# Transformer layer on one core: rope tables ahead of the token tiles, first key norm behind the second tile's splitting

## The chip, the cores and the metric

The kernel runs on one core of a Trainium2 chip. The metric is the device time of one execution in microseconds (us). A core has TensorE (PE: matrix products, whose results go to PSUM banks; PEld are its weight loads), VectorE (DVE), ScalarE (ACT), GpSimd (POOL) and SyncE (SP), which issues nearly all the transfers here. The engines run their own instruction lists and wait for one another through semaphores.

## The reference, cut to what matters

One layer over 1024 latent tokens of width 1024 and 256 context tokens, all in float32:

```python
sh1, sc1, g1, sh2, sc2, g2 = modulation(c, w_mod, b_mod)          # silu(c) @ w_mod + b_mod, also for c_ctx
h_lat = rmsnorm(x, g_attn) * (1 + sc1) + sh1                      # context tokens: with their own shift and scale
z = h @ w_in                                                      # parts cq 256, ckv 128, kr 32, qs 512, ks 128, vs 128
q_m = rmsnorm(rmsnorm(cq, g_q_a) @ w_uq, g_mla_q)                 # 8 heads of 64 + 32
kv  = rmsnorm(ckv, g_kv_a) @ w_ukv                                # 8 heads: 64 for the key, 64 value
k_m = rmsnorm(concat(k_nope, broadcast(kr)), g_mla_k)
q_s, k_s = rmsnorm(qs, g_swa_q), rmsnorm(ks, g_swa_k)             # 8 heads and 2 heads of 64
# latent tokens: rotary embedding of the last 32 of q_m and k_m, and of q_s and k_s
mix = concat(mla_latent(...), swa_latent(...)); x = x + g1 * (mix @ w_out)
x = x + g2 * (relu(modulate(x) @ w_mlp1) ** 2 @ w_mlp2)
```

## The kernel before, in words

The kernel has four stages one after the other: tokens, attention, output projection, MLP. Only the token stage is touched. It ends near 240 us of 1422.

**Precision.** Products are made in three passes. Each float32 operand is split: a high part (ACT copies it into a type with fewer mantissa bits, F32R) and a low part (DVE subtracts: operand less high part), and TensorE sums high x high, high x low and low x high. So each weight has a job `high_weights(j)` on ACT and `low_weights(j)` on DVE; the jobs, in the order of `JOBS` (L264), are a0 and a1 (rows 0 to 3 and 4 to 7 of the 416 columns that keys and values come from), kv (w_ukv), r0 to r3 (a quarter each of the 768 other columns of w_in) and uq (w_uq). The low part of a0 is made by POOL (L455), counted on the semaphore `first_low`. The others are counted on `w_lo`. Each transposed tile is split in the same way by `hi_fill` (ACT) and `lo_fill` (DVE).

**Tiles.** The 1280 tokens are ten tiles of 128, tiles 0 and 1 context (`lat(t)` is false), 2 to 9 latent. What happens to a tile t:

- `square_x` (ACT) sums the squares, then root and inverse. For tiles 0 and 1 `root_x` and `inverse_x` do that for the tile alone, in `stx`. For a later tile its sum goes into column 26 of `stn` and takes part in the root and inverse of the norms of tile t - 2 (`variances`, `roots`, `inverses`).
- `scale_x` (DVE) multiplies with inverse and scale row; `add_shift` (POOL) adds the shift row. Tile 0 has `modulate_first` on DVE for both, straight from PSUM.
- TensorE transposes the tile in two halves (`fill` x0, x1), both are split, and `project(t, 0)` gives the 416 columns; latent tiles have `project(t, 1)` and `(t, 2)` for the other 768.
- `copy_z` takes the result to SBUF, `take_a` squares parts of it. The compressed part is transposed and split (`c`), and `up_kv` (latent: also `up_q`) multiplies with w_ukv (w_uq).
- Norm: `square_k`, `variances`, `roots`, `inverses`, then `scale_s`, `scale_q`, `scale_k`, `high_v` and `low_v`. POOL rotates (`rotate_keys`, `rotate_queries`) and spreads the rotated key over the heads (`widen_key`).
- The results are transposed again (`fill` s, sk, k0, k1, q0, q1), split, and stored to DRAM (`spill_...`).

**Order.** The order of each engine's work is written out by hand, as a loop over i from 0 to 10 in `gpsimd`, `scalar`, `vector` and `tensor`, with lap i making the projection of tile i and finishing tile i - 1. All transposes take turns in PSUM banks 0 and 1, in the order of `slot`: a transpose may start when the one two before it has been split (semaphore `emptied`). The tile 0 keys (sk, k0, k1 of 0) are transposed in lap 2, between the products of `project(2, 0)`. In lap 0, `spread_row(n)` makes TensorE copy scale and shift rows over all partitions; 0 to 3 are for context, 4 to 7 for latent tiles; `copy_spread(n)` brings them to SBUF, from the banks in `spread_bank` (L263). All four latent rows come ahead of tile 0's `fill("c", 0)`.

**Tables.** The cosines and sines come from DRAM (`rope`, 768 KB) and are multiplied on POOL with the norm gains, by `build_table`, three `tensor_tensor` each, for four tables in `tab`: one in lap 0 behind `rotate_keys(0)`, the other three in lap 1 behind `rotate_keys(1)`. The gains that contain the attention scale are made by DVE first (`gains_scaled`).

**Transfers.** `sync` issues, in this order: the column of c, six blocks of w_mod (1 MB each), tile 0, two blocks of w_mod, a0, tile 1, a1, norm columns and rows (`gains`), kv, r0, r1, rope, r2, r3, uq, then tiles as their buffer comes free and the results.

## Time and profile before

| | |
|---|---|
| median of 3 runs | 1425.94 us (1423.24 to 1425.99) |
| the profiled execution, time | 1423.98 us |
| its span, first to last instruction | 1422.2 us |
| PE busy | 1354.3 us (95%) |
| PEld | 1144.6 us (80%) |
| DVE | 959.3 us (67%) |
| ACT | 703.0 us (49%) |
| POOL | 479.5 us (34%) |
| mean granted TensorE clock | 0.989 |

Times in the rows below are microseconds from the start of the span. In a timeline each line is a run of like instructions of one engine: start, duration from the start of the first to the end of the last, line of the kernel, operation, output <- inputs with their sizes, count, and in square brackets the idle time of the engine just before with what ended it. An engine that sits inside an instruction longer than the operation needs has no idle time in this view. The granted clock is 1.00 for TensorE's 2.4 GHz and 0.50 for 1.2 GHz.

### The profile page before, as it was taken

What the parts mean: (1) busy time and instruction counts of PE and PEld (TensorE: products, weight loads), DVE (VectorE), ACT (ScalarE), POOL (GpSimd) and SP (SyncE); (2) the same over time, 40 slices, a digit from 0 to 9 for tenths busy, and PEclk for the clock granted to TensorE, in tenths of its full rate; (3) what the DMA queues carried; (4) which work ended last, traced back from release to release, by engine and by line L of the source; (5) the groups of instructions that cost most, each with busy time, mean ns of one, the idle gap of its engine ahead of it and who ended that gap; (6) DMA issues with size and microseconds to landing.
All of it is one profiled execution on the core that took longest, in us unless ns stands there. A gap on an engine that the chain in (4) does not pass through costs nothing.

```text
span 1422.2 us, 18829 instructions
## 1 busy us (share of the span) xinstructions
PE 1354.3 (95%) x7274; PEld 1144.6 (80%) x7274; DVE 959.3 (67%) x1327; ACT 703.0 (49%) x1339; POOL 479.5 (34%) x295
## 2 busy tenths in 40 slices
PE   5799997999999999999999999999999999999969
PEld 1588886888788998998888888888888888888857
DVE  1888776888877877785774646557465656637477
ACT  2656655777778776972223424333233324323321
POOL 2666563000099992501002304132140503223060
PEclk9899999999999999999999999999999999999989
DMA  9465657900146556201123112121210212121003
GB/s 376 153 176 167 163 170 253 279 1 1 51 169 204 182 145 188 69 1 45 45 65 128 30 30 89 30 74 30 89 30 15 89 30 76 29 89 30 30 29 119
DMA packets 116969, 141.33 MB, mean 99 GB/s; under 512 B 7672, under 2 KB 98680, under 8 KB 114064
## 3 DMA queue, kind: packets, MB, share of 16 engines
q1 hardware_dynamic: 116624, 140.08, 31.5%
q8 instruction: 58, 0.95, 0.3%
q14 instruction: 31, 0.25, 0.1%
q0 software_dynamic: 256, 0.05, 0.0%
HBM read 108.37 MB, written 31.74 MB: 99 GB/s over the span
## 4 chain that ended last, share of the span: by engine, by line
PE 75%; DVE 11%; ACT 9%; DMA 2%; issue 2%; SPq 0%; DVEq 0%; ACTq 0%
PE f_ps L2024 24%; PE f_ps L2259 21%; PE a_ps L1381 7%; PE o_ps L1736 6%; PE a_ps L1397 6%; PE a_ps L1425 5%; ACT s_pr L1476 3%; PE t_ps L943 2%; ACT s_pT L1486 2%; PE t_ps L932 2%; DMA t_wm<-in_w_mod 1%; DVE s_nmx L1559 1%; PE t_ps L958 1%; ACT l_pr L1493 1%; DVE l_nb L1564 1%
## 5 line engine op out<-in xcount | busy, mean ns | idle before, releaser
L2024 PE MATMUL f_ps<-h,f_w 128*128 128x512 f32 x1536 | 357.9, 389 | 0.4 <-DVE h L1802 0.3
L2024 PEld LDWEIGHTS f_ps<-h,f_w 128*128 128x128 f32 x1536 | 288.1, 188 | 60.7 <-DVE h L1802 0.7
L2186 DVE TENSOR_TENSOR mix<-mix,f_ps 128x512 f32<-128x512 f32 x208 | 136.3, 683 | 149.6 <-PE f_ps L2259 149.6
L2067 POOL TENSOR_TENSOR f_w<-f_w,f_g 128x1024 f32<-128x1024 f32 x32 | 81.8, 2577 | 393.2 <-DMA f_w<-in_w_mlp 345.8
L2259 PE MATMUL f_ps<-f_bh,f_ah 128*128 128x512 f32 x448 | 175.4, 391 | 13.2 <-DVE mix L2186 13.1
L2259 PE MATMUL f_ps<-f_bh,f_al 128*128 128x512 f32 x448 | 175.0, 391 | 0.0
L2259 PE MATMUL f_ps<-f_bl,f_ah 128*128 128x512 f32 x448 | 175.0, 391 | 0.0
L2104 ACT ACTIVATE f_a<-f_ps 128x512 f32<-128x512 f32 x64 | 38.2, 597 | 254.7 <-PE f_ps L2024 254.7
L1573 DVE TENSOR_TENSOR l_pT<-a_ps,l_pT 128x512 fp32r<-128x512 f32 (+1 forms) x192 | 109.0, 594 | 53.0 <-ACT l_pT L1486 52.9
L1381 PE MATMUL a_ps<-l_k,l_q 96*128 96x512 f32 (+1 forms) x576 | 136.4, 366 | 0.5 <-DVE l_mo L1594 0.5
L943 PE MATMUL t_ps<-w_in,t_h 128*128 128x416 f32 (+2 forms) x600 | 123.6, 351 | 0.0
L1486 ACT ACTIVATE l_pT<-a_ps 128x512 fp32r<-128x512 f32 (+1 forms) x192 | 95.0, 525 | 39.2 <-PE a_ps L1397 38.8
L2259 PEld LDWEIGHTS f_ps<-f_bh,f_ah 128*128 128x128 f32 x448 | 84.6, 189 | 31.6 <-issue 14.0
L1493 ACT ACTIVATE l_pr<-a_ps,l_nb 128x256 f32<-128x256 f32 (+1 forms) x128 | 100.4, 789 | 13.9 <-DVE l_nb L1564 11.4
L2158 DVE TENSOR_TENSOR f_al<-f_a,f_ah 128x1024 fp32r<-128x1024 f32 x40 | 61.5, 1538 | 66.5 <-ACT f_ah L2115 66.5
L1381 PEld LDWEIGHTS a_ps<-l_k,l_q 96*128 96x128 f32 x576 | 95.3, 189 | 12.4 <-DVE l_mo L1594 0.7
L943 PEld LDWEIGHTS t_ps<-w_in,t_h 128*128 128x128 f32 x600 | 97.5, 189 | 6.1 <-DVE t_h L717 0.5
L2259 PEld LDWEIGHTS f_ps<-f_bl,f_ah 128*128 128x128 f32 x448 | 84.7, 189 | 17.5
L2259 PEld LDWEIGHTS f_ps<-f_bh,f_al 128*128 128x128 f32 x448 | 84.5, 189 | 17.7
L1564 DVE TENSOR_REDUCE l_nb<-a_ps 128x1 f32<-128x1280 f32 x64 | 94.8, 1482 | 3.9 <-PE a_ps L1381 3.4
L1397 PE MATMUL a_ps<-ident,l_pr 128*128 128x128 f32 x640 | 94.3, 275 | 2.4 <-DVE l_pT L1573 1.4
L1425 PE MATMUL a_ps<-l_pT,l_v 128*128 128x256 f32 x640 | 91.4, 289 | 1.1 <-DVE mix L1587 0.6
(212 smaller groups left out, 2355.2 us busy)
## 6 DMA issues: line engine op xcount, KB each, us to landing
l_wg<-in_w_mod SPq DMA_DIRECT2D x8, 2048.0 KB, 8.5
f_w1r<-in_w_mlp SPq DMA_DIRECT2D x32, 512.0 KB, 4.1
f_w<-in_w_mlp SPq DMA_DIRECT2D x16, 1024.0 KB, 5.0
t_wm<-in_w_mod SPq DMA_DIRECT2D x8, 1024.0 KB, 12.7
scratch_k<-t_kT SPq DMA_DIRECT2D x20, 384.0 KB, 4.3
l_k<-scratch_k SPq DMA_DIRECT2D x8, 960.0 KB, 9.7
scratch_q<-t_qT SPq DMA_DIRECT2D x16, 384.0 KB, 5.0
l_q<-scratch_q SPq DMA_DIRECT2D x8, 768.0 KB, 6.6
```

Source lines behind the costliest of these rows:

```text
L943: ins = MM(ps[:, ZB + n % 2, 0:w], hT[a][:, k, :], w_in[x][:, k, ZC[c]], start=(k == 0 and i == 0), stop=(k == KC - 1 and i == 2))
L1381: last = MM(fps[:, a0:a0 + hi - lo], qT[b][:, a, qt * P:(qt + 1) * P], kT[b][:, w, lo:hi], start=(i == 0), stop=(i == 2))
L1397: last = nc.tensor.transpose(ps[:, TB + n % 2, c * P:(c + 1) * P], x, ident[:, :])
L1425: last = MM(ps[:, OB, 0:2 * P], vm[h % 2][:, t, :], flat(l_pT[half][:, u % 2, t, :, :]), start=(half == 0 and t == 0), stop=(half == 1 and ...
L1486: nc.scalar.activation(hi_lo(s, k)[0], turned(s, k), ACT.Copy).then_inc(hi_ready, 1)
L1493: nc.scalar.activation(l_pr[:, odd, lo:hi], fps[:, a0 + lo:a0 + hi], ACT.Exp, bias=nb[:, odd:odd + 1], accum_out=l_sums[:, i, m % NB, m // ...
L1564: V.tensor_reduce(nb[:, s % 2:s % 2 + 1], fps[:, (s % 2) * KALL:(s % 2 + 1) * KALL], AX.X, ALU.max, negate=True).then_inc(shift_ready, 1)
L1573: V.tensor_tensor(lo, turned(s, k), hi.bitcast(F32), ALU.subtract).then_inc(emptied, 1)
L1736: last = nc.tensor.matmul(ps[:, YB[t % 2] + half, :], mT[:, t % 2, a, k, :], w_out[w][:, k, half * BANK:(half + 1) * BANK], start=(k == 0 ...
L2024: last = nc.tensor.matmul(ps[:, b, :], w1[:, g % 2, w, k, :], h2[x][:, k, half * HB:(half + 1) * HB], start=(k == 0 and i == 0), stop=(k = ...
L2186: V.tensor_tensor(y, x, ps[:, bank_of(d, i, t), :].rearrange("p (k c) -> p k c", c=P), ALU.add).then_inc(added, 1)
L2259: last = nc.tensor.matmul(ps[:, b, :], op_a[s][x][:, f, t * P:(t + 1) * P], op_b[s][w][:, f, :], start=(i in (M1, M2, M5) and f == 0 and k ...
```

## The change

- SP: norm columns and rows ahead of the last two blocks of w_mod; rope ahead of kv, r0 and r1.
- POOL: all four tables before the loop, behind waits for `rope_loaded` and `gains_scaled`; the low part of a0 is no longer POOL's; in lap 1 `add_shift(2)` stands ahead of `widen_key(0)`.
- DVE: the gains are scaled ahead of the modulation row; the low part of a0 stands between the modulation row and `modulate_first`; in lap 0 the low part of r0, now behind the splitting of tile 1, an `inverse_x(2)` of its own and `scale_x(2)` stand ahead of the low part of r1; the norm of tile 0 (`finish(0)`) moves from the start of lap 1 to behind the splitting of tile 2, and the low part of r2 behind it.
- ACT: latent rows 6 and 7 are copied behind the splitting of tile 1; tile 2 gets `root_x(2)`; `square_k(0)`, `roots(0)`, `high_v(0)` and then the high part of r2 stand behind the splitting of tile 2.
- PE: rows 6 and 7 behind `up_kv(0)`, in banks 4 and 5; the keys of tile 0 behind k = 5, 6 and 7 of `project(2, 0)` (before: 1, 3 and 5).

```diff
-    stx = small("t_stx", [P, 2])
+    stx = small("t_stx", [P, 3])
-    spread_bank = (5, 6, 7, 3, 4, 5, 6, 7)
+    spread_bank = (5, 6, 7, 3, 4, 5, 4, 5)
@@ sync
         load_x(0)
+        sp.dma_start(cols[:, :], A["norm_cols"]).then_inc(gains, 16)
+        sp.dma_start(norms[:, :], A["norm_rows"]).then_inc(gains, 16)
         load_wm(KC - 2)
         load_wm(KC - 1)
         load_raw("a0")
         load_x(1)
         load_raw("a1")
-        sp.dma_start(cols[:, :], A["norm_cols"]).then_inc(gains, 16)
-        sp.dma_start(norms[:, :], A["norm_rows"]).then_inc(gains, 16)
+        sp.dma_start(rope[:, :, :], A["rope_rows"]).then_inc(rope_loaded, 16)
         load_raw("kv")
         load_raw("r0")
         load_raw("r1")
-        sp.dma_start(rope[:, :, :], A["rope_rows"]).then_inc(rope_loaded, 16)
@@ gpsimd
-        pool.wait_ge(w_hi, 1)
-        G.tensor_tensor(split_view("a0", 1), raw_view("a0"), split_view("a0", 0).bitcast(F32), ALU.subtract).then_inc(first_low, 1)
         pool.wait_ge(gains, 32)
...
+        pool.wait_ge(rope_loaded, 16)
+        pool.wait_ge(gains_scaled, 1)
+        build_table(0, 64, ROPE, b_mk[:, NOPE:QK])
+        build_table(2 * ROPE, 256, SD, b_sk)
+        build_table(2 * ROPE, 128, SD, b_sq)
+        build_table(0, 0, ROPE, b_mq[:, NOPE:QK])
         for i in range(NT + 1):
+            if i == 1:
+                add_shift(2)
             if i:
...
                 widen_key(i - 1)
-            if i + 1 < NT:
+            if i != 1 and i + 1 < NT:
                 add_shift(i + 1)
             if i < NT:
                 rotate_keys(i)
-            if i == 0:
-                pool.wait_ge(rope_loaded, 16)
-                build_table(0, 64, ROPE, b_mk[:, NOPE:QK])
-            if i == 1:
-                pool.wait_ge(gains_scaled, 1)
-                build_table(2 * ROPE, 256, SD, b_sk)
-                build_table(2 * ROPE, 128, SD, b_sq)
-                build_table(0, 0, ROPE, b_mq[:, NOPE:QK])
@@ scalar, the loop
-            if i:
+            if i > 1:
                 square_k(i - 1)
...
-            if i:
+            if i > 1:
                 roots(i - 1)
                 high_v(i - 1)
...
             if i == 0:
-                for n in range(4, 8):
-                    copy_spread(n)
-            if i == 1:
-                high_weights("r2")
+                copy_spread(4)
+                copy_spread(5)
...
             if i == 0:
-                square_x(2, stn[:, 0, 26:27])
+                copy_spread(6)
+                copy_spread(7)
+                square_x(2, stx[:, 2:3])
+                root_x(2)
                 high_weights("r1")
             if i == 1:
+                square_k(0)
+                roots(0)
+                high_v(0)
+                high_weights("r2")
                 high_weights("r3")
                 high_weights("uq")
@@ vector
+        def finish(t):
+            link.reach()
+            variances(t)
+            inverses(t)
+            scale_s(t)
+            if lat(t):
+                scale_q(t)
+            scale_k(t)
+            low_v(t)
         inverse_x(0)
+        (the three scalings of the gains, gains_scaled)
         dve.wait_ge(wm_used, KC)
...
         V.tensor_tensor(mo[:, :], mo[:, :], gm, ALU.mult).then_inc(mod_ready, 1)
+        dve.wait_ge(w_hi, 1)
+        V.tensor_tensor(split_view("a0", 1), raw_view("a0"), split_view("a0", 0).bitcast(F32), ALU.subtract).then_inc(first_low, 1)
         modulate_first()
...
         scale_x(1)
-        (the three scalings of the gains, gains_scaled)
         low_weights("kv")
         for i in range(NT + 1):
...
-            if i:
-                (the lines of finish(i - 1), with scale_x(2) behind inverses for i == 1)
+            if i > 1:
+                finish(i - 1)
             if 1 < i < NT - 1:
                 scale_x(i + 1)
-            if i < 2:
-                low_weights(("r0", "r2")[i])
...
             if i + 1 < NT:
                 lo_fill("x0", i + 1)
                 lo_fill("x1", i + 1)
-            if i < 2:
-                low_weights(("r1", "r3")[i])
+            if i == 0:
+                low_weights("r0")
+                inverse_x(2)
+                scale_x(2)
+                low_weights("r1")
             if i == 1:
+                finish(0)
+                low_weights("r2")
+                low_weights("r3")
                 low_weights("uq")
@@ tensor, the loop
-                project(i, 0, {1: ("sk", 0), 3: ("k0", 0), 5: ("k1", 0)} if i == NCT else {})
+                project(i, 0, {5: ("sk", 0), 6: ("k0", 0), 7: ("k1", 0)} if i == NCT else {})
             if i == 0:
-                for n in range(4, 8):
-                    spread_row(n)
+                spread_row(4)
+                spread_row(5)
...
-                    pe.wait_ge(spread_copied, 8)
+                pe.wait_ge(spread_copied, 8 if i else 4)
                 pe.wait_ge(emptied, slot["c", i] + 1)
                 up_kv(i)
+                if i == 0:
+                    spread_row(6)
+                    spread_row(7)
```

## Rows read from the trace of the kernel before

**Rows 1.** Chain of waits in order of time: start, duration, engine, tile, line.

```profile
66.14 3.39 DVE w_uq L705 x2
```

**Rows 2.** Timeline of TensorE: start, us, operation, count, idle time before it.

```profile
39.74 3.59 PE L990 MATMUL t_ps<-t_mo,ident 128*128 128x512 f32 x8
...
47.79 4.81 PE L943 MATMUL t_ps<-w_in,t_h 128*128 128x416 f32 x24
...
58.65 1.09 PE L932 MATMUL t_ps<-ident,t_x 128*128 128x128 f32 x4 [4.13 <-POOL t_x L404]
...
61.59 2.91 PE L971 MATMUL t_ps<-w_kv,t_c 128*128 128x512 f32 x6
64.30 1.61 PE L943 MATMUL t_ps<-w_in,t_h 128*128 128x416 f32 x6
...
69.92 0.64 PE L932 MATMUL t_ps<-ident,t_kn 128*96 128x128 f32 x4 [1.10 <-DVE t_sK L728]
...
74.58 0.41 PE L932 MATMUL t_ps<-ident,t_sn 128*128 128x128 f32 x2 [1.13 <-DVE t_sn L768]
...
87.05 5.78 PE L943 MATMUL t_ps<-w_in,t_h 128*128 128x416 f32 x33
```

**Rows 3.** Timeline of GpSimd (POOL), 30 to 73 us.

```profile
30.06 3.73 POOL L455 TENSOR_TENSOR w_in<-w_in_raw,w_in 128x1664 fp32r<-128x1664 f32 x1 [24.89 <-ACT w_in L494]
...
39.86 2.37 POOL L404 TENSOR_TENSOR t_x<-t_x,t_shift_c 128x1024 f32<-128x1024 f32 x1 [5.75 <-DVE t_x L685]
42.19 1.24 POOL L392 TENSOR_TENSOR t_krot<-t_z,t_tab 128x32 f32<-128x32 f32 x1
43.39 1.73 POOL L393 TENSOR_TENSOR t_krs<-t_z,t_tab 128x16 f32<-128x16 f32 x1
...
47.27 1.58 POOL L440 TENSOR_TENSOR t_tab<-t_rope,t_norms 128x256 f32<-128x256 f32 x3
...
62.55 9.91 POOL L440 TENSOR_TENSOR t_tab<-t_rope,t_norms 128x512 f32<-128x512 f32 x9
```

**Rows 4.** Timeline of VectorE (DVE), 35 to 70 us.

```profile
35.42 0.69 DVE L717 TENSOR_TENSOR t_h<-t_ps,t_h 128x512 fp32r<-128x512 f32 x1 [0.38 <-ACT t_h L511]
...
36.63 1.89 DVE L708 TENSOR_TENSOR w_in<-w_in_raw,w_in 128x1664 fp32r<-128x1664 f32 x1
...
39.93 3.38 DVE L701 SCALAR_TENSOR_TENSOR w_kv<-w_kv_raw,t_cols,w_kv 128x1024 fp32r<-128x1024 f32 x1
43.24 1.80 DVE L708 TENSOR_TENSOR w_in<-w_in_raw,w_in 128x1536 fp32r<-128x1536 f32 x1
...
49.45 1.76 DVE L708 TENSOR_TENSOR w_in<-w_in_raw,w_in 128x1536 fp32r<-128x1536 f32 x1 [1.72 <-ACT w_in L494]
51.13 0.68 DVE L742 TENSOR_REDUCE t_stn<-t_sqk 128x8 f32<-128x512 f32 x1
...
53.09 1.28 DVE L685 SCALAR_TENSOR_TENSOR t_x<-t_x,t_inv,t_scale_l 128x1024 f32<-128x1024 f32 x1
...
55.36 0.87 DVE L787 SCALAR_TENSOR_TENSOR t_vm<-t_ps,t_inv,t_vm 128x256 fp32r<-128x256 f32 x2
...
66.07 3.47 DVE L705 SCALAR_TENSOR_TENSOR w_uq<-w_uq_raw,t_cols,w_uq 128x768 fp32r<-128x768 f32 x2
```

**Rows 5.** Issue of the table's source (SP timeline), then its landing (DMA view).

```profile
26.96 1.01 SPq L355 DMA_DIRECT2D t_rope<-in_rope_rows  x1
...
t_rope<-in_rope_rows SPq DMA_DIRECT2D x1, 768.0 KB, 12.2
```

**Rows 6.** Stretches: busy per engine, TensorE clock, DMA share, GB/s.

```profile
35.00:40.00 5.00, 4.90 (x25) 4.79 (x26) 4.32 (x10) 4.18 (x8) 0.14 (x1) 1.00 1.02 411
...
60.00:65.00 5.00, 4.18 (x13) 3.58 (x14) 3.41 (x9) 3.39 (x5) 4.77 (x11) 0.50 0.08 28
65.00:70.00 5.00, 3.90 (x24) 3.43 (x23) 5.00 (x5) 3.13 (x7) 4.92 (x3) 1.00 0.00 0
```

**Rows 7.** Timeline of ScalarE (ACT): the square of tile 2.

```profile
46.90 1.05 ACT L480 ACTIVATE t_junk<-t_x 128x1024 bf16<-128x1024 f32 x1
```

More of the change, by code:

```diff
@@ L678, in scale_x @@
         def scale_x(t):
-            r = stx[:, t:t + 1] if t < 2 else inv[:, (t - 2) % 2, 26:27]
+            r = stx[:, t:t + 1] if t <= NCT else inv[:, (t - 2) % 2, 26:27]
             scale = scale_l if lat(t) else scale_c
@@ L828, in vector @@
         inverse_x(0)
+        dve.wait_ge(gains, 32)
+        dve.wait_ge(cleared, 7)
+        V.scalar_tensor_tensor(out=g_qk[0:NOPE, :], in0=cols[0:NOPE, 3:4], scalar=MLA_SCALE, in1=cols[0:NOPE, 4:5],
+                               op0=ALU.mult, op1=ALU.mult)
+        V.tensor_scalar(b_mq, b_mq, MLA_SCALE, None, ALU.mult)
+        V.tensor_scalar(b_sq, b_sq, SWA_SCALE, None, ALU.mult).then_inc(gains_scaled, 1)
         dve.wait_ge(wm_used, KC)
@@ L837, in vector @@
         scale_x(1)
-        dve.wait_ge(gains, 32)
-        dve.wait_ge(cleared, 7)
-        V.scalar_tensor_tensor(out=g_qk[0:NOPE, :], in0=cols[0:NOPE, 3:4], scalar=MLA_SCALE, in1=cols[0:NOPE, 4:5],
-                               op0=ALU.mult, op1=ALU.mult)
-        V.tensor_scalar(b_mq, b_mq, MLA_SCALE, None, ALU.mult)
-        V.tensor_scalar(b_sq, b_sq, SWA_SCALE, None, ALU.mult).then_inc(gains_scaled, 1)
         low_weights("kv")
@@ L849, in vector @@
                 lo_fill("k1", 0)
-            if i:
-                link.reach()
-                variances(i - 1)
-                inverses(i - 1)
-                if i == 1:
-                    scale_x(2)
-                scale_s(i - 1)
-                if lat(i - 1):
-                    scale_q(i - 1)
-                scale_k(i - 1)
-                low_v(i - 1)
+            if i > 1:
+                finish(i - 1)
             if 1 < i < NT - 1:
                 scale_x(i + 1)
-            if i < 2:
-                low_weights(("r0", "r2")[i])
             if i == 4:
```

## The prediction, made before the changed kernel ran

> **What bounds the kernel now.** I read first the table by engine and the 40 slices: TensorE (PE) is busy 95% of the span, and the only thin part besides the load of the modulation weights is the first tenth. Then the chain of waits, in order of time: from 87 us on it runs lap after lap over TensorE with small joints, while between 36 and 76 us it runs mostly over VectorE (DVE) splitting weights [rows 1]. Then TensorE's timeline of that stretch. The reader is to see its gaps: 4.13 us before the first transpose of tile 2, which waits for GpSimd's (POOL's) shift of that tile, 1.10 us at 69.92 before the transposes of tile 0's keys, second half, and 1.13 us at 74.58 before those of tile 1; from 87.05 the laps of latent tiles are full [rows 2]. The question for the whole change is therefore one number: by how much does the start of the fourth tile, 87.05, move? Behind it the same instructions follow in the same order, with no lap that could give time back.
>
> Last I read POOL and VectorE side by side. POOL's shift of tile 1 runs 39.86 to 42.23; VectorE's kv low part is entered at 39.93 and takes 3.38 us. POOL's next, an operation on 32 elements, takes 1.24 us and ends as that low part does; the one after it, on 16 elements, takes 1.73 us and ends with VectorE's r0 low part [rows 3, 4]. They take turns, one whole instruction each. The r1 low part at 49.45, with POOL idle, takes 1.76 us. And nine table products take 9.91 us at 62.55, where their own pace would give 6.9 (below), with 3.5 us of low parts of r3 and uq beside them: 6.9 + 3.5 = 10.4. Turns explain this; running beside each other doesn't.
>
> **The change part by part.**
>
> *DMA order.* The table's source landed at 26.96 + 12.2 = 39.2 us [rows 5]. It now has w_ukv and two quarters of w_in_r less ahead of it, 0.52 + 2 x 0.79 = 2.10 MB, at 411 GB/s [rows 6] 5.1 us: it lands at 34.1. Norm rows and columns (0.16 MB) go ahead of the last two modulation blocks: 0.4 us, I take 0.5 with the small packets, for everything on the modulation's path. SP issues all this some 10 us ahead of its landing, so its queue loses nothing.
>
> *Low part of a0 from POOL to VectorE.* It goes ahead of the first tile's modulation. Its high part is ready at about 30.4 (0.5 later); 1.9 us as for a1 [rows 4]; modulation can start at 32.35 instead of 30.7. The first tile is then transposed and split 1.4 us later, and the a1 low part starts at 38.1 instead of 36.63. POOL is rid of 3.73 us [rows 3], but it had nothing to do then. This 1.4 us is covered by what follows, which is later still; uncovered it would cost 1.4.
>
> *Tables ahead of the tiles: the main term.* All twelve products now stand on POOL before the shift of tile 1. Their pace, start to start: the first three (256, 128 and 128 elements) took 1.58 us; I take 0.70 for 256, 0.42 for 128 and 1.25 for 512. 2 x 1.25 + 6 x 0.70 + 4 x 0.42 = 8.4, with the joints 8.6. Alone that is 34.2 to 42.8. But VectorE enters four operations with both inputs in SBUF in that stretch: a1 low 1.75, kv low 1.1 (3.38 less the 2.3 that it stood), scaling of tile 1, as many elements, 1.1 once it has its turn, vs low 0.2: 4.15 us. By turns, the tables end at 46.9 and the shift of tile 1 (2.37) at 49.3. Before it ended at 42.23: 7.1 us later. Bounds: 45.2 with no turns at all; 50.3 if the rotation's small operations get between too.
>
> *What waits for it.* TensorE has the spread rows 4 and 5 (1.7) behind the first tile's projection, which ends at 41.1 with its 1.2 to 1.4 of delay, then tile 0's transpose, done at 43.3, then nothing for 6 us. In the idle time of the kernel before the clock fell to 0.50 (1.2 GHz), and it was back at 1.00 only after 65 us, when TensorE had worked almost without a gap since 60.82 [rows 2, 6]. So I take half clock from 49.3 to about 54: two transposes 1.1 us each (the row at 58.65), the kv product 2.7 (61.59 to 64.30) against the half of its 2.91 us row, some 1.5, at full clock, two spread rows 1.7 (four took 3.59 with the last one's tail). 49.3 + 2.2 + 2.6 + 1.7 = 55.8 for the start of tile 1's projection, which was 47.79. Here the two spread rows, moved behind kv, stand in front of the projection, and their copies on ScalarE (ACT) in front of the square of tile 2.
>
> *The second tile's chain and tile 2.* Spread row 7 is copied by 56.3; the square of tile 2 takes 1.2 [rows 7]; its root and inverse, now steps of their own, 0.6 (tile 1's stood between the split that ends at 36.11 and the a1 low part at 36.63); scaling 1.28 [rows 4]: 59.4, against 54.37 before. Then POOL's shift and the low part of r1 start together. POOL first: shift done at 61.8; VectorE first: 63.5. Before, the transposes behind it started at 58.65 [rows 2]. Tile 1's projection (4.8 us) ends at 60.6, so from there TensorE waits. Transposes, splitting and the kv product of tile 1 follow; tile 2's projection starts at 66.6 or 68.4, I take the middle, 67.5, against 64.30.
>
> *Norm of tile 0 behind the splitting.* VectorE is through with tile 2's splitting at about 66.8, a little ahead of the projection. The norm of tile 0 takes 3.8 us: from 51.13 to 56.23 less the 1.28 of scaling in between [rows 4]. Then r2 and r3, 1.76 each, and uq: 3.47 less the 1.75 in which two table products had the turn = 1.7. That is 9.0, with half a microsecond for turns with POOL's key rotation: 76.3; then the low part of the sK tile, 0.4: 76.7. TensorE needs that before it can transpose the second half of tile 0's keys, now after k = 7 of tile 2's projection, and everything behind it, the key norm of tile 1 as well, comes from here. Before it was 69.92. So 6.7 us later. From 69.92 to 87.05 the order of the work stays as it was, with the same waits (next late is tile 1's key norm for the transposes at 74.58, 4.66 us behind, as before).
>
> **Sum.** 87.05 becomes 93.8: +6.7 us. The profiled execution took 1423.98 (span 1422.2 and 1.8 around it); with 6.7 it is 1430.7. The median shown is 1425.94, 2.0 above that execution, so I state 1425.94 + 6.7 = **1432.6**.
>
> **The skill, weighed.** The VectorE rows above show turns with low parts that are plain tensor_tensor operations on fp32 [rows 3, 4]. The Trainium skill, "Advanced Engine Details and Errata", section VectorE Performance Modes, puts the interference on 2-port Vector instructions and lists tensor_tensor as having no such mode: by it the low parts and the tables would run side by side. "SBUF — State Buffer" of the Trainium skill, section on the two sides of SBUF, calls it an exclusive lock held for the whole instruction and counts in operations with two SBUF inputs. The traces bear out the second. What the first would make of the time is rival one.
>
> **Rivals.**
> 1. *No turns during the tables.* POOL's products or VectorE's operations slip past each other. Then tables to 42.8, shift to 45.2 (3.0 later than before), TensorE idle for 2 us only and at full clock, two transposes 1.3, kv 1.5, two rows 1.8: projection 1 at 49.8; copy 7 at 50.4, scaling of tile 2 done at 53.5, shift at 55.8 or 57.6; VectorE through with tile 2's splitting at 60.3 in either case (the low part of r1 stands there anyway). Plus 3.8 + 5.2 + 0.4 = 69.7, against 69.92. No change: 1425.7. For it: only that page. Against: three rows with durations of two to four times the operation's own and more. It is the bound on the good side of the main term.
> 2. *The splitting gains: faster.* One mechanism: before, VectorE's norm of tile 0 and the low parts of r2 stood between scaling and splitting, and TensorE sat 4.13 us waiting for tile 2. If the shift of tile 2 is done by 54 us, VectorE is through with its splitting by 57.5, and 57.5 + 3.8 + 5.2 + 0.4 = 66.9, 3.0 before 69.92: 1422.9. It decides at the end of the tables: each microsecond later than 40 us takes one of the three. For it: those waits are there. Against: the source doesn't land before 34 and the products alone need 8.6, so it needs products or a landing faster than any row shows.
> 3. *Worse.* VectorE first each time, half clock a second time in the wait for tile 2, POOL's rotations of tile 1 each behind a low part (as the 1.73 us row): 68.4 instead of 67.5, 1 us more of turns, 0.8 of clock: +9.5, 1435.4.
>
> **How the numbers follow.** Forecast (+5 to +8.5) 0.62, rival 1 0.13, rival 2 0.08, rival 3 0.09; 0.08 for something between rival 1 and the forecast (+3 to +5). 0.2% is 2.85 us, about what a measurement of this kernel can tell from no change. Slower takes the forecast, rival 3 and the part between: 0.79; same 0.13; faster 0.08. The forecast's own range is 1430.9 to 1434.5; the one given, 1425.2 to 1436, takes in rival 1.
>
> **What would show it.** Right: table products from about 34 us, some of 2 us and more, in turns with a1, the scaling and kv; shift of tile 1 ending near 49; a gap of some 6 us on TensorE before the first transpose of tile 1, clock 0.50 behind it; tile 1's projection at about 56; the low parts of r2, r3 and uq in a row up to 76; tile 3's projection at about 94. Wrong: tables done by 43, or a gap under 3 us there, or the keys of tile 0 transposed before 72; wrong as a whole if 87.05 hasn't moved by 3 us or if laps behind it have changed length.

## The result, and the profile after

The changed kernel is slower: 1430.69 us in the median of 7 runs (1427.81 to 1432.31), the kernel before 1425.99 (1423.24 to 1428.33, 7 runs beside it). The ratio is 1.0035 [1.0024, 1.0046], 5.0 us [3.4, 6.6]. Measured again with the last experiments it was 1.0036 [1.0023, 1.0050]. The prediction was 1432.6, +6.7: the direction is right, and the loss lies at the lower edge of the forecast's own +5 to +8.5 (1430.69 is just under its 1430.9).

The profiled execution of the changed kernel took 1432.31 us, span 1430.5, mean clock 0.978; that of the kernel before had span 1422.2 and clock 0.989. The 8.3 us between the spans are more than the kernels differ by: the changed kernel's profile is the slowest of its seven executions, the other's is faster than its median. I use the traces for places, the ratios for sizes.

TensorE's timeline of the changed kernel (start, duration, operation, count, idle time before it):

```profile
26.61 1.94 PE L989 MATMUL t_ps<-t_wm,silu 128*32 128x512 f32 x8 [0.58 <-DMA t_wm<-in_w_mod]
30.18 5.18 PE L1000 MATMUL t_ps<-t_mo,ident 128*128 128x512 f32 x8 [1.63 <-DVE t_mo L850]
...
37.21 3.29 PE L1014 MATMUL t_ps<-w_in,t_h 128*128 128x416 f32 x16 [0.34 <-DVE t_h L720]
...
48.83 1.94 PE L942 MATMUL t_ps<-ident,t_x 128*128 128x128 f32 x8 [4.47 <-POOL t_x L404]
50.42 2.91 PE L981 MATMUL t_ps<-w_kv,t_c 128*128 128x512 f32 x6
53.13 2.17 PE L1000 MATMUL t_ps<-t_mo,ident 128*128 128x512 f32 x4
54.73 5.09 PE L953 MATMUL t_ps<-w_in,t_h 128*128 128x416 f32 x24
...
62.92 1.11 PE L942 MATMUL t_ps<-ident,t_x 128*128 128x128 f32 x8 [2.01 <-POOL t_x L404]
63.79 2.77 PE L981 MATMUL t_ps<-w_kv,t_c 128*128 128x512 f32 x6
66.36 4.03 PE L953 MATMUL t_ps<-w_in,t_h 128*128 128x416 f32 x18
...
75.22 1.09 PE L942 MATMUL t_ps<-ident,t_kn 128*96 128x128 f32 x4 [3.06 <-DVE t_sK L731]
75.96 3.55 PE L953 MATMUL t_ps<-w_in,t_h 128*128 128x256 f32 x15
80.32 0.66 PE L942 MATMUL t_ps<-ident,t_sn 128*128 128x128 f32 x2 [0.81 <-DVE t_sn L771]
80.63 4.42 PE L953 MATMUL t_ps<-w_in,t_h 128*128 128x256 f32 x15
...
94.65 5.54 PE L953 MATMUL t_ps<-w_in,t_h 128*128 128x416 f32 x31
```

Read it against [rows 2]. Two waits have changed for the worse: there is now one of 4.47 us for the shift of tile 1, and the one for the sK low part, 1.10 us before, is 3.06 at 75.22. The wait for tile 2 has gone from 4.13 to 2.01. The fourth tile starts at 94.65, before at 87.05. GpSimd shows why tile 1 is late, VectorE what took turns with it, and what stands ahead of the sK tile:

```profile
34.05 12.21 POOL L440 TENSOR_TENSOR t_tab<-t_rope,t_norms 128x256 f32<-128x256 f32 x12 [11.97 <-DMA t_rope<-in_rope_rows]
46.33 2.35 POOL L404 TENSOR_TENSOR t_x<-t_x,t_shift_c 128x1024 f32<-128x1024 f32 x1
...
58.99 3.79 POOL L404 TENSOR_TENSOR t_x<-t_x,t_shift_l 128x1024 f32<-128x1024 f32 x1 [7.77 <-DVE t_x L688]
```

```profile
38.75 2.72 DVE L711 TENSOR_TENSOR w_in<-w_in_raw,w_in 128x1664 fp32r<-128x1664 f32 x1
41.39 1.75 DVE L688 SCALAR_TENSOR_TENSOR t_x<-t_x,t_stx,t_scale_c 128x1024 f32<-128x1024 f32 x1
43.06 1.74 DVE L704 SCALAR_TENSOR_TENSOR w_kv<-w_kv_raw,t_cols,w_kv 128x1024 fp32r<-128x1024 f32 x1
...
58.82 1.75 DVE L711 TENSOR_TENSOR w_in<-w_in_raw,w_in 128x1536 fp32r<-128x1536 f32 x1
...
69.50 3.47 DVE L711 TENSOR_TENSOR w_in<-w_in_raw,w_in 128x1536 fp32r<-128x1536 f32 x2
72.90 1.94 DVE L708 SCALAR_TENSOR_TENSOR w_uq<-w_uq_raw,t_cols,w_uq 128x768 fp32r<-128x768 f32 x2
74.76 0.41 DVE L731 TENSOR_TENSOR t_sK<-t_ps,t_sK 128x256 fp32r<-128x256 f32 x1
```

The chain of waits of the changed kernel (start, duration, what) goes through just these:

```profile
18.22 15.70 DMA t_rope<-in_rope_rows
...
46.33 2.36 POOL t_x L404
...
58.99 3.80 POOL t_x L404
...
69.59 3.39 DVE w_in L711 x2
72.98 1.86 DVE w_uq L708 x2
```

Stretches of the changed kernel (busy us per engine with counts, then the granted clock, DMA share, GB/s):

```profile
20.00:25.00 5.00, 2.63 (x16) 0.20 (x8) 0.69 (x5) 2.63 (x4) 0.38 (x2) 0.50 1.03 422
...
70.00:75.00 5.00, 2.17 (x15) 1.71 (x13) 5.00 (x5) 4.82 (x9) 4.87 (x4) 0.92 0.44 131
75.00:80.00 5.00, 4.29 (x19) 3.97 (x19) 3.36 (x10) 1.49 (x4) 1.47 (x4) 0.50 0.41 106
80.00:85.00 5.00, 4.68 (x18) 4.18 (x19) 4.89 (x8) 2.64 (x11) 2.52 (x2) 0.56 1.01 281
```

and the kernel before, in the same columns:

```profile
20.00:25.00 5.00, 3.17 (x16) 0.38 (x16) 0.32 (x2) 2.63 (x4) 0.00 (x0) 1.00 1.00 414
...
80.00:85.00 5.00, 5.00 (x32) 4.44 (x31) 3.17 (x7) 3.14 (x7) 3.53 (x10) 1.00 0.37 95
```

The changed kernel has half clock (0.50, 1.2 GHz) in two stretches where the kernel before had full clock: during the modulation products, and behind the keys of tile 0. Neither was in the prediction.

### The profile page after: what moved, and what is told of

Same layout as the page of the kernel before. It is cut to its first block, busy times and chain, and to the rows that moved or that the text cites. A ratio compares the mean times of both kernels' runs of the same rounds, so it can differ in the third digit from the quotient of the medians.

```text
span 1430.5 us, 18832 instructions
## 1 busy us (share of the span) xinstructions
PE 1362.8 (95%) x7274; PEld 1152.7 (81%) x7274; DVE 955.7 (67%) x1330; ACT 704.0 (49%) x1340; POOL 478.9 (33%) x294
## 4 chain that ended last, share of the span: by engine, by line
PE 75%; DVE 10%; ACT 8%; DMA 2%; issue 2%; SPq 1%; POOL 1%; DVEq 0%; ACTq 0%; POOLq 0%
PE f_ps L2037 24%; PE f_ps L2272 21%; PE a_ps L1394 7%; PE o_ps L1749 6%; PE a_ps L1410 6%; PE a_ps L1438 5%; ACT s_pr L1489 3%; PE t_ps L953 2%; ACT s_pT L1499 2%; PE t_ps L942 2%; DVE s_nmx L1572 1%; DMA t_rope<-in_rope_rows 1%; PE t_ps L968 1%; ACT l_pr L1506 1%; POOL t_tab L440 1%
## 5 line engine op out<-in xcount | busy, mean ns | idle before, releaser
L953 PE MATMUL t_ps<-w_in,t_h 128*128 128x416 f32 (+2 forms) x600 | 127.3, 359 | 0.0
L953 PEld LDWEIGHTS t_ps<-w_in,t_h 128*128 128x128 f32 x600 | 100.7, 196 | 6.3 <-issue 0.5
```

The source lines that it names most:

```text
L953: ins = MM(ps[:, ZB + n % 2, 0:w], hT[a][:, k, :], w_in[x][:, k, ZC[c]], start=(k == 0 and i == 0), stop=(k == KC - 1 and i == 2))
```

## The experiments

Two theories stood at the outset. By the prediction's, all of the loss comes from the tables ahead of the tiles, and the norm of tile 0 behind the splitting only passes it on. By its rival, the norm's new place costs something of its own. A third came up with the traces: that the norm rows ahead of the last modulation blocks bring on the half clock at the start. Twelve kernels ran, four on the same chip each time, most of them 12 times. Ratios are against the kernel before on that chip (medians 1425.63, 1425.72 and 1424.56 us). One microsecond is 0.0007.

### Tables back in the laps

```diff
@@ gpsimd
-        pool.wait_ge(rope_loaded, 16)
-        pool.wait_ge(gains_scaled, 1)
-        build_table(0, 64, ROPE, b_mk[:, NOPE:QK])
...
         for i in range(NT + 1):
...
                 rotate_keys(i)
+            if i == 0:
+                pool.wait_ge(rope_loaded, 16)
+                build_table(0, 64, ROPE, b_mk[:, NOPE:QK])
+            if i == 1:
+                pool.wait_ge(gains_scaled, 1)
+                build_table(2 * ROPE, 256, SD, b_sk)
+                build_table(2 * ROPE, 128, SD, b_sq)
+                build_table(0, 0, ROPE, b_mq[:, NOPE:QK])
```

> The changed kernel with the four tables built where they were before (one behind the first tile's key rotation, three behind the second's), all else changed. Theory (the tables ahead of tile 1's shift are the cost, by taking turns with VectorE's low parts and by standing in front): the shift of tile 1 ends at about 44 us instead of 48.7, tile 1's projection starts near 49 instead of 54.7, the second half of tile 0's keys is transposed near 71 instead of 75.2 (the three tables now take turns with the low parts of r2, r3 and uq): about 1427, 3 to 5 us under the changed kernel. Rival (the moved norm of tile 0 and the low part of a0 on VectorE are the cost, and the tables are hidden): within 1 us of the changed kernel, 1430.7.

Measured: 1428.40 us (1425.31 to 1432.16, 12 runs), 1.0022 [1.0010, 1.0035]. By the ratios only 1.9 us of the 5.0 come back, and the two intervals overlap; 3.1 us of loss stay, clear of zero. Tile 1's projection starts at 49.07 (changed: 54.73), so the tables' chain is gone, but the loss isn't. TensorE waits behind it:

```profile
70.04 0.64 PE L944 MATMUL t_ps<-ident,t_kn 128*96 128x128 f32 x4 [3.55 <-DVE t_sK L733]
...
77.04 0.66 PE L944 MATMUL t_ps<-ident,t_sn 128*128 128x128 f32 x2 [3.61 <-DVE t_sn L773]
```

Three tables now run on GpSimd from 71.35 to 78.39, beside tile 1's key norm on VectorE, and delay that in turn.

### Tables ahead, and nothing else

```diff
@@ the kernel before; sync and the scaling of the gains as in the changed kernel; gpsimd
+        pool.wait_ge(rope_loaded, 16)
+        pool.wait_ge(gains_scaled, 1)
+        build_table(0, 64, ROPE, b_mk[:, NOPE:QK])
...
         for i in range(NT + 1):
...
                 rotate_keys(i)
-            if i == 0:
-                pool.wait_ge(rope_loaded, 16)
-                build_table(0, 64, ROPE, b_mk[:, NOPE:QK])
...
```

> The kernel before with only the tables ahead of the tile loop, and what they need for it: norm rows and table source earlier in SP's order, and the gains scaled ahead of the modulation row. Norm of tile 0, spread rows and low part of a0 as before. Theory: the tables delay the shift of tile 1 by 6 us, tile 1's projection starts near 54, three tables less stand beside the low parts of r3 and uq (2 us back): 1430 to 1431, the loss of the whole change. Rival (the moved norm is what costs): within 1 us of before, 1426.

Measured: 1428.08 us (1426.80 to 1429.64, 11 runs), 1.0023 [1.0014, 1.0032]: 3.3 us. Tables from 34.47 to 48.18, shift of tile 1 done at 50.60, tile 1's projection at 54.31. It is slower on its own, but by less than the loss of the whole change, 1430 to 1431, that I expected here.

### Tables early, made from the norm rows

This kernel leaves out the cosines and sines, and with them the wait for their transfer:

```diff
-        pool.wait_ge(rope_loaded, 16)
-            G.tensor_tensor(..., rope[:, :, src + o:src + o + w], mid(g, NB), ALU.mult)
+            G.tensor_tensor(..., mid(norms[:, o:o + w], NB), mid(g, NB), ALU.mult)
```

> The changed kernel with the table products made from the norm rows, which land at 21.6 us, in place of the cosines and sines: same number, size and place of products, but they start at about 24 us, when VectorE is nearly idle (so the output isn't the reference's). Theory of turns: the twelve take about 8.6 us plus at most one low part (a0, 1.9) and the modulation row's product (0.7), against 12.2; POOL is free by 35, tile 1's shift ends near 43.5, and the whole is 6 to 8 us under the changed kernel, about 1423.5. Rival (no turns, a table product is slow for its broadcast operand or its strided output): 12.2 us again at 24, still done by 36.5, same gain of time but the group's length tells. Rival (tables are not the cost): 1430.7.

Measured: 1428.07 us (1423.48 to 1430.06, 12 runs), 1.0015 [1.0003, 1.0027]. The tables are out of the way before tile 1, and 2.1 us of loss stay, where I had expected none. This execution also gives the tables' own pace. GpSimd, then VectorE beside it:

```profile
24.33 10.68 POOL L440 TENSOR_TENSOR t_tab<-t_norms 128x256 f32<-128x256 f32 x12 [2.47 <-DVE t_norms L846]
```

```profile
29.11 1.37 DVE L849 TENSOR_TENSOR t_mo<-t_mo,t_bg 128x512 f32<-128x512 f32 x1
30.41 2.41 DVE L851 TENSOR_TENSOR w_in<-w_in_raw,w_in 128x1664 fp32r<-128x1664 f32 x1
```

Taken one by one, the products that meet no such VectorE operation last about 0.72, 0.45 and 1.27 us (256, 128 and 512 elements) in this kernel and in the changed one; from start to start that makes 8.6 us for the twelve, the prediction's figure. So the turns cost GpSimd 2.1 us here and 3.6 in the changed kernel. VectorE's operations beside them last, alone, 2.6 (0.69 and 1.89) and 4.75 (1.89, 1.28, 1.28 and 0.30). They do take turns, and each turn costs GpSimd 0.2 to 0.4 us less than VectorE's operation lasts alone: the product entered at 31.03, beside the low part of a0 (1.89), stood 2.37 us for its 0.72. The other theory, a product slow for its operands, is out.

### Low part of a0 back on GpSimd

```diff
@@ gpsimd, ahead of the tables
+        pool.wait_ge(w_hi, 1)
+        G.tensor_tensor(split_view("a0", 1), raw_view("a0"), split_view("a0", 0).bitcast(F32), ALU.subtract).then_inc(first_low, 1)
@@ vector, ahead of modulate_first
-        dve.wait_ge(w_hi, 1)
-        V.tensor_tensor(split_view("a0", 1), raw_view("a0"), split_view("a0", 0).bitcast(F32), ALU.subtract).then_inc(first_low, 1)
```

> The changed kernel with the low part of a0 back on POOL, ahead of the tables, which start when their source has landed at 34. Theory: the modulation of tile 0 starts 1.5 to 2 us earlier, but the tables end as late as before, since VectorE's a1 low part, scaling and kv low part still take their turns in them, so nothing moves: within 1 us of the changed kernel. Rival (the early delay of 1.4 us is carried to the end): 1.5 to 2 us under it, 1429.

Measured: 1429.17 us (1427.99 to 1430.49, 9 runs), 1.0023 [1.0012, 1.0035]; the changed kernel's interval, [1.0024, 1.0046], overlaps it. Tables at 34.24 (12.19 us) and tile 1's projection at 55.23, as in the changed kernel. By these traces the 1.4 us are hidden at tile 1. In time it isn't settled: the ratios differ by 1.7 us, 1429.17 is the number of the rival, and the overlap of the intervals leaves room for either.

### The norm of tile 0 behind the splitting, and nothing else

Cut to the lines of VectorE that stay changed:

```diff
@@ the changed kernel; transfers, tables, scaling of the gains and low part of a0 as in the kernel before
             if i == 1:
                 finish(0)
                 low_weights("r2")
                 low_weights("r3")
                 low_weights("uq")
```

> The changed kernel with tables, low part of a0, scaling of the gains and order of the transfers all as before. What stays of the change: the norm of tile 0 and the low parts of r2 and r3 behind the second tile's splitting, tile 2's own inverse ahead of r1, the latent spread rows 6 and 7 behind kv, and the later keys of tile 0. Theory (tables and transfers are the loss): tile 0's first product at 35.1, tile 1's projection at 46.5 to 47, the keys' second half near 67, then a gap before tile 1's keys for the tables beside r2, r3 and uq: 1425 to 1427, no change against before. Rival (the norm move makes TensorE wait in one piece of 3 us for r2, r3 and uq, and the half clock behind it costs 2 us): 1427.5 to 1428.5.

Measured: 1429.20 us (1424.29 to 1431.70, 12 runs), 1.0014 [0.9999, 1.0029]: 2.0 us, just short of shown by itself, though the two kernels above that keep this move without the tables' chain both show a loss clear of zero (1.0022, 1.0015). Its trace starts as the kernel before does, at 35.19, so it can be laid beside [rows 2] directly:

```profile
59.23 3.54 PE L955 MATMUL t_ps<-w_in,t_h 128*128 128x416 f32 x18
...
68.46 0.83 PE L944 MATMUL t_ps<-ident,t_kn 128*96 128x128 f32 x4 [3.91 <-DVE t_sK L735]
68.95 3.47 PE L955 MATMUL t_ps<-w_in,t_h 128*128 128x256 f32 x15
75.48 0.55 PE L944 MATMUL t_ps<-ident,t_sn 128*128 128x128 f32 x2 [3.06 <-DVE t_sn L775]
75.68 4.21 PE L955 MATMUL t_ps<-w_in,t_h 128*128 128x256 f32 x15
...
89.45 5.78 PE L955 MATMUL t_ps<-w_in,t_h 128*128 128x416 f32 x33
```

Tile 2's projection comes 5.1 us earlier (59.23 for 64.30) and the second half of tile 0's keys 1.5 us earlier (68.46 for 69.92). That is the gain the change can have been after. From there to the fourth tile it takes 20.99 us, before 17.13. Of these 3.9 us more, 2.4 come before the transposes of tile 1 (7.02 us behind the keys, before 4.66), whose norm takes turns with nine table products; and 1.5 come from half clock: the 15 products behind them take 4.21 us, before 2.72.

### Three tables in the idle time behind the shift of tile 2

```diff
@@ the norm move alone, gpsimd
             if i == 1:
                 add_shift(2)
+                pool.wait_ge(gains_scaled, 1)
+                build_table(2 * ROPE, 256, SD, b_sk)
+                build_table(2 * ROPE, 128, SD, b_sq)
+                build_table(0, 0, ROPE, b_mq[:, NOPE:QK])
...
                 rotate_keys(i)
...
-            if i == 1:
-                pool.wait_ge(gains_scaled, 1)
...
```

> The kernel of the norm move alone, with one table behind the first tile's key rotation and three right behind the shift of tile 2, where POOL had 5 to 6 us with nothing to do. Theory: no table stands in front of a shift and none beside the low parts of r2, r3 and uq, so fourth tile's projection starts at 85 to 87: 1423 to 1426, at or a little under the kernel before, 1 to 2 us under the norm move alone. Rival (the three tables still running when the rotated keys of tile 0 are wanted, or the half clock behind the wait for r2, r3, uq): no gain over the norm move alone.

Measured: 1426.64 us (1423.82 to 1429.66, 12 runs), 1.0005 [0.9992, 1.0018]. The wait for tile 1's transposes falls to 0.81, but the tables (55.20, 7.18 us) stretch tile 0's norm instead: keys at 69.61, and half clock behind them in its trace. No change is shown against the kernel before.

### And the low part of uq behind tile 0's keys

```diff
@@ with the edit above, vector; scalar with high_weights likewise
                 low_weights("r3")
-                low_weights("uq")
...
                 lo_fill("k1", 0)
+                low_weights("uq")
```

> The same as the kernel with the tables in the gaps, and the high and low part of uq behind the splitting of tile 0's keys, so that TensorE's wait for the second half of those keys is 1.8 us shorter. Theory: that wait falls from 3 us to about 1.2, the clock stays at 1.00 behind it: 1.8 to 4 us under it, 1420 to 1423. Rival (uq then stands in front of tile 1's norm, and TensorE waits there instead): no change.

Measured: 1429.17 us (1425.13 to 1432.69, 12 runs), 1.0021 [1.0008, 1.0033]. The wait for the sK tile fell to 2.47 us, and the one behind it grew to 4.34. The uq low part waited 0.90 us for its high part and then stood in front of tile 1's key norm:

```profile
72.87 1.94 DVE L711 SCALAR_TENSOR_TENSOR w_uq<-w_uq_raw,t_cols,w_uq 128x768 fp32r<-128x768 f32 x2 [0.90 <-ACT w_uq L492]
```

### Norm rows ahead, and nothing else

```diff
@@ the kernel before, sync
         load_x(0)
+        sp.dma_start(cols[:, :], A["norm_cols"]).then_inc(gains, 16)
+        sp.dma_start(norms[:, :], A["norm_rows"]).then_inc(gains, 16)
         load_wm(KC - 2)
...
-        sp.dma_start(cols[:, :], A["norm_cols"]).then_inc(gains, 16)
-        sp.dma_start(norms[:, :], A["norm_rows"]).then_inc(gains, 16)
         load_raw("kv")
```

> The kernel before with one edit: the norm columns and rows are sent ahead of the last two blocks of w_mod. Theory A (only their bytes count): everything behind the modulation row moves by 0.5 us, the granted clock stays at 1.00 from 20 to 35 us as in the kernel before, 1426.1. Theory B (they widen TensorE's wait ahead of the seventh block from 1.8 to 2.4 us, and the clock falls to 0.50 with it, as in the changed kernel and all four variants so far): the eight passes of the first spread rows take 5.2 to 5.8 us instead of 3.7, tile 0's first product starts near 37.2 instead of 35.1, and the whole is 1 to 2 us over the kernel before, 1427.5.

Measured: 1426.59 us (1421.88 to 1428.58, 12 runs), 1.0000 [0.9988, 1.0012]. The 0.5 us of this edit don't show. Its trace had the half clock at the start, and is the best picture of what this does to the kernel before:

```profile
30.12 5.99 PE L990 MATMUL t_ps<-t_mo,ident 128*128 128x512 f32 x8 [1.70 <-DVE t_mo L831]
...
37.96 3.29 PE L1004 MATMUL t_ps<-w_in,t_h 128*128 128x416 f32 x16 [0.34 <-DVE t_h L717]
...
50.65 4.81 PE L943 MATMUL t_ps<-w_in,t_h 128*128 128x416 f32 x24
...
89.85 1.47 PE L943 MATMUL t_ps<-w_in,t_h 128*128 128x416 f32 x7
```

The first product is 2.86 us later than in [rows 2]'s execution (35.10 there), tile 1's projection 2.86, the fourth tile 2.80. As far as this trace goes, the kernel before passes a late start on in full to the fourth tile.

### Three more versions of the kernel before

```diff
@@ (1) and (2): the kernel before, vector
-            if i == 1:
-                low_weights("uq")
...
                 c_variances(i)
+            if i == NCT:
+                low_weights("uq")
@@ (2) and (3): the kernel before, gpsimd
             if i == 0:
                 pool.wait_ge(rope_loaded, 16)
                 build_table(0, 64, ROPE, b_mk[:, NOPE:QK])
+                pool.wait_ge(gains_scaled, 1)
+                build_table(2 * ROPE, 256, SD, b_sk)
+                build_table(0, 0, ROPE, b_mq[:, NOPE:QK])
             if i == 1:
-                pool.wait_ge(gains_scaled, 1)
-                build_table(2 * ROPE, 256, SD, b_sk)
                 build_table(2 * ROPE, 128, SD, b_sq)
-                build_table(0, 0, ROPE, b_mq[:, NOPE:QK])
```

> The kernel before with one edit: the low part of uq on VectorE moves from ahead of the splitting of tile 0's keys to ahead of the splitting of tile 3. Theory (what sets the start of the fourth tile is VectorE's row of low parts in front of those keys, 3.5 us of it for uq with its turns): the wait at 69.92 goes, tile 1's keys are transposed 2.5 to 3.5 us earlier, about 1 us is given back where uq stands now: 1.5 to 2.5 us under the kernel before, 1423.5. Rival (the tables, which then stand beside r3 and in front of tile 1's norm, set the start): no change.

> The same, and in addition two more of the tables (k of the windowed heads, q of the latent heads) in lap 0 behind the first, where POOL had 6.7 us with nothing to do, so that only one is left beside the low parts of r3: 0 to 1.5 us under the kernel with uq alone, 1422.5. Rival (they run into the r1 low part and the shift of tile 2, which is on the chain): 0 to 1 us over it.

> The kernel before with only the two tables moved into that gap in lap 0. Theory of turns: the low parts of r3 and uq lose up to 2 us of standing, the shift of tile 2 starts up to 1 us later: 0 to 1.5 us under the kernel before, 1425. Rival (no turns): no change at all, since no other engine waits for the tables.

Measured, 12 runs each: (1) 1426.23 us, 1.0005 [0.9995, 1.0016]; (2) 1426.54, 1.0015 [1.0003, 1.0026]; (3) 1425.91, 1.0012 [1.0000, 1.0023]. In (1) and (2) the low part of uq goes ahead of the splitting of tile 3, in (2) and (3) two more tables stand in lap 0. In (1) the wait for the sK tile is gone and comes back a lap later, as 1.20 us in front of the product with w_uq:

```profile
85.45 2.32 PE L958 MATMUL t_ps<-w_uq,t_c 128*128 128x384 f32 x12 [1.20 <-issue]
```

In (2) the nine products on GpSimd (48.96, 7.45 us), which was idle there, stretch VectorE's scaling and low part, and the shift of tile 2 starts at 59.28, in (1) at 57.88.

### The changed kernel again

> The changed kernel once more, beside the next three. Theory: tables ahead (2.9 us over the kernel before, alone) and the norm move (2.0 us, alone) add up: 1.0035 of before, 1430.5, within 1 us. In its profile the clock between 20 and 35 us may be at 1.00 or at 0.50, whatever the kernel; where it is at 1.00, tile 0's first product starts near 35.5 and the fourth tile's projection near 93; where it is at 0.50, near 37.2 and 94.5.

Measured: 1429.98 us (1428.41 to 1431.98, 6 runs), 1.0036 [1.0023, 1.0050]. Its trace:

```profile
38.29 3.29 PE L1014 MATMUL t_ps<-w_in,t_h 128*128 128x416 f32 x16 [0.34 <-DVE t_h L720]
...
53.88 5.10 PE L953 MATMUL t_ps<-w_in,t_h 128*128 128x416 f32 x24
...
74.42 0.64 PE L942 MATMUL t_ps<-ident,t_kn 128*96 128x128 f32 x4 [3.10 <-DVE t_sK L731]
...
79.25 4.24 PE L953 MATMUL t_ps<-w_in,t_h 128*128 128x256 f32 x15
...
93.08 3.19 PE L953 MATMUL t_ps<-w_in,t_h 128*128 128x416 f32 x16
```

It starts 1.1 us later than the first execution and is ahead of it at tile 1: here the start doesn't count, since the tables' chain hangs on the landing of their source (the tables start at 33.94, in the first execution at 34.05), not on TensorE.

## Why the prediction was right, and where not

TensorE's starts in us, from the traces above:

| | first product | projection 1 | projection 2 | keys, 2nd half | fourth tile |
|---|---|---|---|---|---|
| before, its profile | 35.10 | 47.79 | 64.30 | 69.92 | 87.05 |
| before with norm rows ahead, late start | 37.96 | 50.65 | 67.16 | 72.78 | 89.85 |
| changed | 37.21 | 54.73 | 66.36 | 75.22 | 94.65 |
| changed again | 38.29 | 53.88 | 65.76 | 74.42 | 93.08 |
| predicted for changed | 36.5 | 55.8 | 67.5 | 76.7 | 93.8 |
| tables alone | 37.78 | 54.31 | 69.80 | 74.88 | 91.92 |
| norm move alone | 35.19 | 47.30 | 59.23 | 68.46 | 89.45 |

**DMA order: right.** The table's source landed at 33.92 (18.22 + 15.70), predicted 34.1; the last modulation products started at 26.61, before 26.24, predicted 0.5 later.

**Low part of a0: right as far as the traces show.** 1.89 us ahead of the modulation, and hidden at tile 1; its price in time isn't settled (1.7 us by the ratios, whose intervals overlap).

**Tables: the mechanism right, the size a little high.** Turns with a1, the scaling and kv, as foreseen; 12.21 us for a predicted 12.7, because the turns cost 3.6 us and not 4.15; the products' own 8.6 holds. Shift of tile 1 done at 48.68 (49.3), half clock behind it, projection 1 at 54.73 (55.8). The Trainium skill, "Advanced Engine Details and Errata", section VectorE Performance Modes, names only 2-port Vector instructions as interfering with GpSimd; for fp32 operations with two SBUF inputs the traces show otherwise (a product of 0.72 us stood 2.38 at 39.68, beside the low part of a1). They agree with "SBUF — State Buffer" of the Trainium skill, section on the two separate sides, which counts such operations in. Rival 1 is out: it had the shift done by 45.2.

**Second tile's chain: right.** At tile 2 VectorE went first, the shift took until 62.78 (61.8 or 63.5), projection 2 at 66.36 (67.5).

**Norm and low parts behind the splitting: right.** 9.0 us and 0.5 for turns were predicted; from 65.49 to the end of the uq low part at 74.84 it took 9.35. The keys' second half came at 75.22 for 76.7; 1.3 of the 1.5 us were won ahead of it, where VectorE was through with the splitting at 65.5 instead of 66.8.

**"From 69.92 to 87.05 the order of the work stays as it was, with the same waits": this step failed.** That stretch took 17.13 us before (17.07 with a late start), 19.43 and 18.66 in the two traces of the changed kernel. Nearly all of it is clock. The wait for the sK tile is 3.1 us where it was 1.1, less work is left between it and tile 1's transposes, and the 15 products of 128x256 behind these take 4.2 to 4.5 us in seven of the eight profiles that have the norm behind the splitting, against 2.7 in all six that have it in front (the eighth: 2.72). The forecast counted half clock only for tile 1. The longer wait and the half clock go together in these profiles, but no run changes the wait alone, and the eighth (the low part of a0 back on GpSimd) has the same 3.06 us wait with full clock at these products. So the half clock is shown, its cause isn't.

**"The median is 2.0 above that execution, so I add 6.7 to it": this was unsafe, and probably too high.** The profiled execution of before was unusual by its clock: 0.989, where the median of 97 other executions of that kernel was 0.984 and 92 of them lay at or below 0.987. By its time it wasn't: 31 of the 97 were as fast or faster. In every profile of a changed or experimental kernel but two, the first product came 1.7 to 3.7 us later than its 35.10 (1.4 of it was foreseen where VectorE has the low part of a0). Of the seven profiles whose work is the same up to there, three start at 35.1 to 35.2 and four at 36.8 to 37.7. So it is likely, though not shown, that many executions of the kernel before start late as well: no second profile of that very kernel was taken. With a late start its fourth tile starts near 89.9 rather than 87.05; the changed kernel, whose tile 1 waits for the tables either way, doesn't get later with it. Against the late start the two traces of the changed kernel are 3.2 and 4.8 us behind at the fourth tile.

**How the sum came out.** In the first pair of traces: 6.7, less 1.5 at the keys, plus 2.3 behind them, makes 7.5, where 7.6 us were found at the fourth tile (94.65 for 87.05). A late start of the kernel before takes back up to 2.8 of these. What was measured is 1.7 us (by the ratio) to 1.9 us (by the median) below the forecast. That it is so close is partly luck: the half clock that it lacks (about 2 us) and the late start that it lacks (up to 2.8) stand against each other.

**"Behind it the same instructions follow": true, but they don't take the same time.** From the start of the fourth tile to the end of the span the 14 profiles take 1332.9 to 1337.7 us: 1335.1 in the kernel before, 1335.9 and 1334.5 in the two of the changed kernel. This 4.8 us of scatter is as large as the effect, and doesn't go with any edit that I can name. So the starts in the table say where time is lost; how much of it reaches the end only the ratios say.

**What the loss is made of.** Against the late start: +3.2 to +4.1 at projection 1 from the tables; then the norm's move gives back 1.6 (+1.6 and +2.4 are left at the keys); then the half clock takes another 1.6 to 2.4. The parts alone agree in time: tables 3.3 us [2.0, 4.6], norm move 2.0 [-0.1, 4.1], together 5.3 for 5.0. The part of the tables, with their earlier transfers, is shown; how the rest divides between the norm's move and the low part of a0 is only bounded by these runs. Rival 2 was half right: the splitting does gain, 1.5 us at the keys when it stands alone. It doesn't reach the end: the low parts of r2, r3 and uq in one row make one long wait of several short ones, tile 1's norm then takes turns with the nine table products, and half clock follows. Where those products stood elsewhere (1.0005) the half clock was there all the same.

No version tried is faster than the kernel before; the nearest three (1.0000, 1.0005 and 1.0005) can't be told from it.

## What to carry to other kernels

Before moving work to an idle GpSimd, list what VectorE does beside it with two inputs in SBUF: every such pair seen here takes turns, whole instructions at a time, and the idle engine is no free slot. VectorE's operations with one input in PSUM weren't held up (0.69 us at 36.46 and 37.53, beside table products, as at 35.42 before with GpSimd idle). Moving low-urgency work together turns several short waits of TensorE into one long one, so price what follows that wait at half clock too. Before taking a profile as the base of a sum, compare its mean clock with that of the other executions; a delay at the start counts for a kernel whose chain runs through TensorE, and not for one that waits for a transfer. And don't read a difference of a few us from the spans of two profiles: here the untouched part alone varies by 4.8.

## What the runs showed of the hardware that I had not expected

The clock fell in the modulation stage, where TensorE waits for each block: 0.50 from 20 to 30 us in the changed kernel, with 2.63 and 2.97 us of 5 busy, while the kernel before had 1.00 there with 3.17 and 2.73 busy. The eight copies of spread rows behind it then take 5.2 to 6.4 us instead of 3.67. I took the norm rows' transfer for the cause. But the three experiments with the old order of transfers on the kernel before start at 36.79 to 37.65 as well, and the norm rows alone cost no time that shows (1.0000), so that theory is not borne out. Of the 14 profiles, 13 have 0.50 in some stretch from 20 to 30 us; in two of them (the norm move alone and the one with three tables behind the shift) it was back at 1.00 before the spread rows, and their first product isn't late. What decides when it falls and comes back stays open.

In the second run of the changed kernel the clock stayed at full through a 3.10 us wait at 74.42 and fell behind the next (2.24 us); in the first it fell behind the 3.06 us wait itself. Executions of one kernel differ: the 97 of the kernel before lie between 1421.5 and 1429.1 us, so that 0.1% needs more than the dozen runs taken here.

Small operations suffer most from the turns: GpSimd's rotations of 32 and 16 elements, 0.25 and 0.22 us alone at 48.64, take 1.69 and 1.73 beside VectorE's low parts at 69.67, and VectorE's tensor_scalar operations on 8 columns beside table products took 0.77 instead of 0.22.
